# A hybrid decoder trunk on one core: the state space part with one shared phasor table, and each head's gate, norm and output placed among the next head's pieces

## The reference, cut to what matters

```python
def even_mixer(hn, w_in, ...):
    proj = hn @ w_in                       # 2048 -> 512 + 4*1536
    u, q, k, v, g = split(proj)            # 6 retention heads of 256
    y_s5 = s5_mixer(u, ...)                # 32 groups x 64 complex states
    q, k = apply_rope(q), apply_rope(k) * 256 ** -0.5
    o = retention(q, k, v, gamma_log)      # decayed causal scores, 2 chunks of 128
    o = o * rsqrt(mean(o * o, -1) + EPS) * ret_norm
    return concat([y_s5, silu(g) * o]) @ w_out

def s5_mixer(u, ...):
    dt = exp(log_dt); mag = exp(lr * dt)
    ab = mag * (cos(li * dt) + i sin(li * dt))
    bb = f(ab, lr, li) * b
    bu = einsum(u, bb)
    x = associative_scan(x_t = ab * x_{t-1} + bu_t)      # complex
    y = gelu(Re(c x) + d * u)
    return y * sigmoid(y @ glu_w + glu_b)
```

## Time and profile before

| | |
|---|---|
| median of 3 runs | 2261.57 us (2256.18 to 2261.68) |
| the profiled execution | 2257.0 us, span 2255.2 us |
| PE busy | 2162.7 us (96%) |
| DVE busy | 1471.7 us (65%) |
| ACT busy | 1003.2 us (44%) |
| POOL busy | 776.3 us (34%) |
| first matmul of the output projection of layer 0 | 438.62 us |

### The profile page before, as it was taken

How to read it: one execution, slowest core, us unless ns; L and a number is a source line. 1 busy time by engine, 2 the same in 40 slices (tenths; PEclk the granted TensorE clock), 3 DMA queues, 4 the chain that set the end, 5 groups by cost and what they waited for, 6 DMA issues and landing times.

```text
span 2255.2 us, 47390 instructions
## 1 busy us (share of the span) xinstructions
PE 2162.7 (96%) x18426; PEld 2132.9 (95%) x18426; DVE 1471.7 (65%) x1747; ACT 1003.2 (44%) x1244; POOL 776.3 (34%) x880
## 2 busy tenths in 40 slices
PE   8788888999999999999999999999999999999997
PEld 8788777999999999999999989999999999999997
DVE  6378766577666655666666666677666555666666
ACT  4243333444444444444444445545444444444442
POOL 5799995023434300433411000023443101443311
PEclk9899998999999999999999999999999999999999
DMA  6334233454555456555455533455554556554553
GB/s 262 114 135 154 98 135 125 158 201 178 207 200 187 166 193 221 196 194 186 176 187 198 192 125 123 162 192 188 206 187 174 186 193 220 197 187 185 174 197 114
DMA packets 64604, 398.69 MB, mean 177 GB/s; under 512 B 7169, under 2 KB 9729, under 8 KB 29057
## 3 DMA queue, kind: packets, MB, share of 16 engines
q1 hardware_dynamic: 60192, 391.15, 48.2%
q10 hardware_dynamic: 4320, 6.27, 0.8%
HBM read 395.29 MB, written 2.10 MB: 176 GB/s over the span
## 4 chain that ended last, share of the span: by engine, by line
PE 81%; POOLq 9%; POOL 5%; issue 2%; DVE 2%; ACT 1%; DVEq 0%; DMA 0%; ACTq 0%
PE PS L1401 25%; PE PS L1402 25%; PE PS L1405 25%; POOLq L1288 2%; POOLq L1292 2%; POOL g L1290 2%; POOL E L1293 2%; POOLq L1159 2%; POOLq L1166 1%; PE PS L1396 1%; PE PS L1397 1%; PE PS L1398 1%; POOLq L1306 1%; POOL S L1305 1%; PE PS L1751 0%
## 5 line engine op out<-in xcount | busy, mean ns | idle before, releaser
L705 DVE TENSOR_TENSOR lo<-raw,hi 128x1024 fp32r<-128x1024 f32 (+2 forms) x826 | 950.4, 1170 | 527.0 <-ACT hi L356 521.8
L356 ACT ACTIVATE hi<-raw 128x1024 fp32r<-128x1024 f32 (+2 forms) x826 | 785.8, 969 | 722.2 <-PE PS L1405 676.1
L1401 PE MATMUL PS<-XS,hi 128*128 128x256 f32 x3584 | 851.6, 280 | 8.2 <-ACT hi L356 8.2
L1402 PE MATMUL PS<-XS,hi 128*128 128x256 f32 x3584 | 845.4, 278 | 0.0
L1401 PEld LDWEIGHTS PS<-XS,hi 128*128 128x128 f32 x3584 | 680.2, 190 | 15.8 <-issue 15.4
L1402 PEld LDWEIGHTS PS<-XS,hi 128*128 128x128 f32 x3584 | 680.4, 190 | 0.4
L1405 PE MATMUL PS<-XS,lo 128*128 128x256 f32 x3584 | 480.8, 277 | 0.0
L1405 PEld LDWEIGHTS PS<-XS,lo 128*128 128x128 f32 x3584 | 441.5, 188 | 0.0
L1401 PE MATMUL PS<-YF,hi 128*128 128x256 f32 x1408 | 331.8, 276 | 0.0
L1402 PE MATMUL PS<-YF,hi 128*128 128x256 f32 x1408 | 331.8, 276 | 0.0
L1358 POOL TENSOR_TENSOR ctmp<-apad,cws 128x512 f32<-128x512 f32 x88 | 131.9, 1519 | 526.0 <-DVE apad L756 526.0
(11 more groups left out here) (238 smaller groups left out, 2487.7 us busy)
## 6 DMA issues: line engine op xcount, KB each, us to landing
raw<-in_ffn_up SPq DMA_DIRECT2D x176, 1024.0 KB, 4.8
raw<-in_ffn_dn SPq DMA_DIRECT2D x128, 704.0 KB, 4.1
raw<-in_w_in SPq DMA_DIRECT2D x51, 1024.0 KB, 4.9
raw<-in_w_oe SPq DMA_DIRECT2D x16, 1024.0 KB, 4.8
raw<-in_w_oo SPq DMA_DIRECT2D x16, 1024.0 KB, 4.8
raw<-in_mla_dn SPq DMA_DIRECT2D x9, 1024.0 KB, 4.8
raw<-in_w_ukv SPq DMA_DIRECT2D x8, 1024.0 KB, 4.8
raw<-in_w_uq SPq DMA_DIRECT2D x8, 768.0 KB, 4.3
```

The lines of the kernel that those rows point to most:

```text
L356: act.activation(hi[:, p % SLOTS, 0:n], raw[:, u % SLOTS, off:off + n], ACT.Copy).then_inc(hi_ready, 1)
L705: V.tensor_tensor(lo[:, p % SLOTS, 0:n], raw[:, u % SLOTS, off:off + n], f(hi[:, p % SLOTS, 0:n]), ALU.subtract).then_inc(lo_ready, 1)
L1401: mm(PS[:, bank, 0:T], wh, x[:, 0:T], start=first, stop=False)
L1402: mm(PS[:, bank, 0:T], wh, x[:, T:2 * T], start=False, stop=False)
```

## The change

1. The S5 setup is divided: POOL keeps the two exponentials (`s5_magnitude`) and the seven squarings (`s5_powers`); DVE gets the angles, the first phasor, the factor and the scaled B, one part after each of head 0's first four splits. The semaphore `den_ready` goes; `th_ready` and `ph_ready` come.
2. The first 32 steps of all 16 columns' phasors are built once (`first_phasors`, in tiles that share their memory with `acc` and `lot`). `phasors` copies its part and makes levels 5 to 7 only.
3. B's transposes move from G's piece 2 to V's piece 3 of head 0, and ACT's copies of them to behind V's copy.
4. In the S5 heads: b_u(0) and b_u(1) after K's pieces 1 and 2, c_x(0) and b_u(2) after V's piece 1, b_u(3) after V's piece 2, and c_x(1) after K's piece 2 of the next head. DVE makes scan(1) after the second of the next head's K splits. POOL makes rotate_in(0) ahead of the change of sign of C, and C is loaded after bu_copy(1).
5. A head's root, SiLU, norm, output and rounding are taken out of its end and stand in the next head's K stage (`root_and_gate`, `round_y`, `gate_and_variance`, `norm_head`, `head_output`, `y_low`), among the splits of its Q pieces. ACT squares the output after the second K split instead of ahead of all four.
6. The prologue's third and fourth sums of squares stand after piece 4, and the first banks of U are scaled ahead of two splits. `sum_squares` gets one drain.

The diff, cut to its core:

```diff
+        acc, lot = sums[:, 0:2, :], sums[:, 2:4, :]
+        E32 = sums[:, :, :].rearrange("p a t -> p (a t)").rearrange("p (a m n) -> p a m n", a=2, m=KD)
...
# scalar, in even_head
                 for i in range(4):
-                    if h0 == 0 or i:
-                        split(p0 + 4 + i, 16, r)
-                    if s5 and i == 1:
-                        bu_copy(0)
+                    split(p0 + 4 + i, 16, r)
+                    if h0 and i == 0:
+                        root_and_gate(r, h0 - 1)
+                    if s5 and i in (1, 2):
+                        bu_copy(i - 1)
+                    if s5 and i == 2:
+                        load_c()
+                    if glu and i == 2:
+                        act.wait_ge(c_done, 8)
+                        act.dma_start(gluw, A["gluw"]).then_inc(gluw_in, 16)
+                if h0:
+                    round_y(r, h0 - 1)
...
-                act.wait_ge(o_done, H_(1, 1))
-                act.activation(sq[:, :, :], PS[:, 5, :].rearrange("p (a t) -> p a t", a=2), ACT.Square).then_inc(osq_ready, 1)
-
                 for i in range(4):
                     split(p0 + 16 + i, 16, r)
+                    if i == 1:
+                        act.wait_ge(o_done, H_(1, 1))
+                        act.activation(sq[:, :, :], PS[:, 5, :].rearrange("p (a t) -> p a t", a=2),
+                                       ACT.Square).then_inc(osq_ready, 1)
...
# vector
+            root(0)
+            scale_banks(U[:, 0:2, :], 7, 0)
             splits(8, kinds=("std",) * 2)
-            scale_banks(U[:, 0:2, :], 7, 0)
...
                 for i in range(4):
-                    if h0 == 0 or i:
-                        split(p0 + 4 + i, 16, r)
+                    if h0 and i == 0:
+                        gate_and_variance(r, h0 - 1)
+                    split(p0 + 4 + i, 16, r)
+                    if h0 == 0:
+                        (s5_angles, s5_phasor, s5_factor, s5_b)[i]()
+                    if h0 and i == 0:
+                        norm_head(r, h0 - 1)
+                    if h0 and i == 1:
+                        head_output(r, h0 - 1)
+                if h0 > 1:
+                    y5()
+                if h0:
+                    y_low(r, h0 - 1)
                 rotate(KRo, p0 + 4, e0)
...
-                if s5:
-                    scan(1)
...
                 for i in range(4):
                     split(p0 + 16 + i, 16, r)
+                    if s5 and i == 1:
+                        scan(1)
...
# gpsimd
+            def double(e, n, lo_, cos_, sin_):
+                pool.drain()
+                c_, s_ = lo_
+                G.tensor_tensor(c_, e[:, :, :, 0:n], cos_, ALU.mult)
+                G.tensor_tensor(s_, e[:, :, :, 0:n], sin_, ALU.mult)
+                pool.drain()
+                G.tensor_tensor(e[:, 0, :, n:2 * n], c_[:, 0], s_[:, 1], ALU.subtract)
+                G.tensor_tensor(e[:, 1, :, n:2 * n], c_[:, 1], s_[:, 0], ALU.add)
+
+            def first_phasors():
+                G.memset(E32[:, 0, :, 0:1], 1.0)
+                G.memset(E32[:, 1, :, 0:1], 0.0)
+                for l in range(5):
+                    n = 1 << l
+                    c, s_ = (ph[:, l, ri, :].unsqueeze(1).unsqueeze(3).broadcast_to([P, 2, KD, n]) for ri in range(2))
+                    double(E32, n, (g1m[:, :, :, 0:n], g2m[:, :, :, 0:n]), c, s_)
+                pool.drain()
...
             def s5_chunk(h0, r):
+                if h0:
+                    stage(h0, r)
                 phasors(0, h0, r)
-                pool.drain()
+                rotate_in(0, h0, r)
                 pool.wait_ge(cst_in, at(16 * h0 + 16, 16, r))
...
-                rotate_in(0, h0, r)
                 phasors(1, h0, r)
                 rotate_in(1, h0, r)
...
-            pool.wait_ge(den_ready, 1)
-            s5_setup()
+            s5_magnitude()
+            s5_powers()
             pool.wait_ge(bank_free, 2)
             pool.wait_ge(bt_ready, 2)
+            stage(0, None)
+            first_phasors()
             s5_chunk(0, None)
...
# tensor
                 def after_k(i):
-                    if s5 and i == 1:
-                        b_u(0)
+                    if h0 > 1 and i == 2:
+                        c_x(1)
+                    if s5 and i in (1, 2):
+                        b_u(i - 1)
...
-                    if s5:
-                        if i == 1:
-                            c_x(0)
-                            b_u(3)
+                    if s5 and i == 1:
+                        c_x(0)
+                        b_u(2)
+                    if s5 and i == 2:
+                        b_u(3)
+                    if i < 2:
+                        after_q(i + 4)
+                    if i == 3 and h0 == 0:
+                        b_transposed()
...
-                        if s5:
-                            c_x(1)
-                    if i == 2 and h0 == 0:
-                        b_transposed()
```

More of the change, by code:

```diff
@@ L290, in build @@
         cneg_ready = sem("cneg_ready")
-        den_ready = sem("den_ready")
         bu_done = sem("bu_done")
@@ L445, in even_head @@
                     act.activation(U[:, :, :], U[:, :, :], ACT.Gelu_apprx_tanh).then_inc(ge_ready, 1)
-                for i in range(4):
-                    split(p0 + 8 + i, 16, r)
-                    if s5 and i == 0:
-                        bu_copy(1)
+                splits(p0 + 8, 16, r)
                 for i in range(4):
                     split(p0 + 12 + i, 16, r)
-                    if s5 and i < 2:
-                        bu_copy(i + 2)
+                    if s5 and i in (1, 2):
+                        bu_copy(i + 1)
                 act.wait_ge(piece_done, at(p0 + 12, 16, r))
@@ L458, in even_head @@
                 act.activation(Vr[:, 0, :], PS[:, pair(e0 + 2), 0:T], ACT.Copy, scale=rtok[:, 0:1]).then_inc(v_ready, 1)
+                if h0 == 0:
+                    act.wait_ge(bt_psum, 8)
+                    for b in range(2):
+                        act.activation(BT[:, 2 * b:2 * b + 2, :, :].rearrange("p a b c -> p (a b c)"),
+                                       PS[:, 6 + b, :], ACT.Copy).then_inc(bt_ready, 1)
                 if glu:
@@ L495, in _ @@
             even_head(None, 5, False, True)
+            root_and_gate(None, 5)
+            round_y(None, 5)
             def out_projection(n, p0):
@@ L787, in lambda_squared, with tt, ts @@
                 dve.drain()
-                V.reciprocal(pt[:, 12, :], pt[:, 13, :]).then_inc(den_ready, 1)
+                V.reciprocal(pt[:, 12, :], pt[:, 13, :])
+            def tt(o, a, b, op):
+                V.tensor_tensor(o, a, b, op)
+                dve.drain()
+            def ts(o, a, s1, s2, o1, o2=None):
+                if o2 is None:
+                    V.tensor_scalar(o, a, s1, None, o1)
+                else:
+                    V.tensor_scalar(o, a, s1, s2, o1, o2)
+                dve.drain()
@@ new lines, in stt, with s5_angles @@
+            def stt(o, a, s, b, o1, o2):
+                V.scalar_tensor_tensor(out=o, in0=a, scalar=s, in1=b, op0=o1, op1=o2)
+                dve.drain()
+            def s5_angles():
+                th, cs, sn, a, b, c = (col(i) for i in (2, 3, 4, 5, 6, 7))
+                dve.wait_ge(th_ready, 1)
+                ts(a, th, 2.0 / math.pi, MAGIC, ALU.mult, ALU.add)
+                ts(a, a, -MAGIC, None, ALU.add)
+                parts, rest = [], math.pi / 2
+                for bits in (8, 9, 10):
+                    scale = 2.0 ** (bits - 1 - math.floor(math.log2(rest)))
+                    v = math.floor(rest * scale) / scale
+                    parts.append(v)
+                    rest -= v
+                parts.append(rest)
+                stt(b, a, -parts[0], th, ALU.mult, ALU.add)
+                for v in parts[1:]:
+                    stt(b, a, -v, b, ALU.mult, ALU.add)
+                tt(c, b, b, ALU.mult)
+                ts(sn, c, 1.0 / 362880, None, ALU.mult)
+                for k in (-5040, 120, -6):
+                    stt(sn, sn, 1.0 / k, c, ALU.add, ALU.mult)
+                stt(sn, sn, 1.0, b, ALU.add, ALU.mult)
+                ts(cs, c, -1.0 / 3628800, None, ALU.mult)
+                for k in (40320, -720, 24, -2):
+                    stt(cs, cs, 1.0 / k, c, ALU.add, ALU.mult)
+                ts(cs, cs, 1.0, None, ALU.add)
@@ new lines, in s5_b @@
+            def s5_b():
+                B, o, w = (x.rearrange("p a b t -> p (a b t)").rearrange("p (a m c) -> p a m c", a=2, m=KD)
+                           for x in (sB, sT1, sT2))
+                fr, fi = (col(i).unsqueeze(2).broadcast_to([P, KD, 32]) for i in (10, 11))
+                tt(o[:, 0], B[:, 0], fr, ALU.mult)
+                tt(w[:, 0], B[:, 1], fi, ALU.mult)
+                tt(o[:, 0], o[:, 0], w[:, 0], ALU.subtract)
+                tt(o[:, 1], B[:, 1], fr, ALU.mult)
+                tt(w[:, 0], B[:, 0], fi, ALU.mult)
```

(6 more changed lines are left out.)

252 lines of the change are left out of this document (110 added, 142 removed).

## The result

The changed kernel takes **2229.05 us** (median of 4 runs, 2228.34 to 2229.64), against 2260.24 for the kernel before on the same chip: a ratio of 0.9865, with a 95% interval of 0.9848 to 0.9882. It is faster by 31 us; 2205 was forecast, with a range up to 2226. The direction was right, the gain was a little over half of what the sum said, and the time lies 3 us outside the range. The profiled execution has a span of 2226.9 us.

A forecast was written before the change was run, and what follows sets the result against it. POOL's chain was taken to bound the S5 heads, with DVE and POOL blocking each other second. Gains of 14 + 28 + 12 = 54 us bring the profiled 2257.0 to 2203, forecast as 2205 us, range 2182 to 2226.

The forecast's parts named there:

- The setup, step by step: Divided S5 setup: B ready at 64 us, PE waits 6 at V0, POOL starts chunk 0 at about 82.
- the table in front of chunk 0: Shared first phasors on POOL, built once before chunk 0's rotation: about 10 us.
- The mutual blocking: DVE instructions with two SBUF inputs and POOL instructions reading SBUF exclude each other for a whole instruction.
- (d): Steady S5 heads: period falls from 68.4 to 59 us (56 to 62), three periods 28 us less.
- (e): Interleaved heads: c_x(0) held about 3 us, G ends 32.7 after rotate_in(0), 6 us of PE waits per head stay.
- (f): Last head: 53.9 us, so 86.6 from the last rotate_in(0) to the output projection, against 98.4.
- rival 2: S5 heads: new chain longer, POOL waits 5 us more per chunk, period 64 to 65; 2225 us, chance 0.22.
- Rival 1: S5 heads: PE becomes the bound as blocking vanishes with the small POOL operations; 2180 us, chance 0.23.
- 14 + 28 + 12 us: Gains before the output projection: first rotate_in(0) earlier, three shorter periods, shorter stretch after the last rotate_in(0).

The follow-up runs named there:

- e6: Changed kernel with 36 useless matmuls put in front of c_x(0), in the place of PE's wait, in heads 1 to 4; 2217.00 us.
- e3: Changed kernel with levels 5 to 7 of every phasor table left out, so the output is not the reference's; 2192.36 us.
- e14: Changed kernel with the shared table before POOL's wait for B, the second half's last level held until scan(0) ended, and scan(0), c_x(0) one piece later; 2207.64 us.
- e10: Changed kernel with POOL's levels for a chunk's second half held back until scan(0) of the same head has ended; 2218.94 us.
- e12: Changed kernel with the shared table before POOL's wait for B and only the second half's largest level held until scan(0) ended; 2218.18 us.
- e4: Changed kernel with one 1.75 us reciprocal added on DVE in the K stage of heads 1 to 4; 2232.27 us.
- e13: Changed kernel with the reciprocal and Newton step of the heads' norm replaced by one product, so the output is not the reference's; 2211.28 us.
- e7: Changed kernel with scan(0) one V split later on DVE, and c_x(0), b_u(2) and b_u(3) one V piece later on PE; 2224.76 us.

## Why the prediction was right and wrong

**What was right.** That nothing changes from the output projection on. The setup, step by step: PE's wait at head 0's first V piece was put at 6 us and is 5.62; the first rotate_in(0) was forecast to end at 121 and ends at 122.2; the table in front of chunk 0 was called a price. The 121 is partly luck: POOL starts chunk 0 at 86.29 in place of 82 and needs 35.9 us from there in place of 39, so two errors of 3 to 4 us cancel. PE's 15.3 us wait is gone. The mutual blocking was seen and named as what decides.

**What failed is step (d), the period of 59, which measured 64.7, and (e), the layout behind rotate_in(0).** The sum in (d) takes DVE's and POOL's exclusive operations, 64 us less 5 (for the 5 there is no row), as if each would always find the other one's work to run against and never an idle engine. That is the period of a well-packed order, and this order isn't one. POOL idles 14.5 us per head, because rotate_in needs b_u copied, b_u stands behind c_x(0) in PE's queue, and c_x(0) waits for scan(0). DVE idles 6.7 us in V and G. Both are then busy together in the K stage and in scan(0), where blocking is paid on the path. The layout by hand had scan(0) end 7.2 us behind rotate_in(0); it ends 15.2 behind it (246.84 to 262.08): 5.9 because DVE, with the norm and two splits of 2.8 us ahead of it, arrives late, and the rest because scan(0) takes 9.4 beside the levels. In place of (e)'s 3 us wait PE waits 5. In head 4 the four G pieces end at 353.20, 41.6 us behind rotate_in(0) in place of 32.7, and head 5 takes 56.3 us in place of the 53.9 of (f).

**What was missing: the clock.** I allowed 1.5 us for it once, in the setup. It costs 3.3 us in each of the heads with c_x(0) (e6), 12 us in all, half of the miss; without it (e6) the period is 61.5, inside the 56 to 62 of (d). The rows to see it from were in the trace of before: the granted clock of 0.93 in an S5 head, where a share of PE's waits was to remain by my own layout.

**The balance of the miss** in the forecast's own terms, 410.19 less 384.6 = 25.6 us: the first rotate_in(0) +1.2; from it to the last one 189.4 in place of 177, +12.4 (the first of the three steps is 60.0, since scan(0) of chunk 0 ends 10.8 us behind its rotate_in(0), the other two 64.7 and 64.8); from the last one to the output projection 98.6 in place of 86.6, +12.0, of which 8.0 lie before the end of scan(0).

**The rivals.** It is rival 2 that came: POOL waiting for b_u(3) behind V's pieces, scan(0) waiting for a DVE that holds the norm, a period of 64 to 65, 2225 us. These orders of waiting are in the trace, its time is 4 us off, and I gave it 0.22 against 0.50. That the number fits so well is luck in part: it had POOL wait 5 us per chunk, POOL waits 14.5 and isn't the bound, and the rival named neither the stretched scan(0) nor the clock, without which the period is 61.5 (e6). Its weight should have come from the order of the queues, which the diff shows: with the norm put in front of scan(0), and bu_copy behind the splits of V, the period can't be that of free packing. Rival 1 (2180) was refuted as argued: PE's rate is only reached when POOL's levels are gone altogether (e3, 2192).

**And the three terms of the gain?** The sum had 14 + 28 + 12 us for start, periods and last stretch. By the places of the table the changed kernel reaches 5.0 (head 1's scores), 12.2 (three heads) and 11.2 (from head 4's scores to head 5's). The 11.2 are no success of (f): from the end of the last rotate_in(0) to head 4's scores 27.9 us pass (311.60 to 339.46), where it took 16.4 before (340.20 to 356.65). e14 reaches 12.5, 27.6 and 11.1. So a gain of the size forecast was within reach of this kernel, with three more edits; that the terms agree doesn't show that each price was right, since e14 gets there with a wait and a clock loss that the forecast didn't have.

The Trainium skill, "SBUF — State Buffer", section "Who interferes with whom", was used for the exclusion. The runs agree, and add that it isn't a loss to be counted once: e10 has the same instructions on both engines, and DVE's busy time differs by 5.5 us per head according to when POOL works.

## What to carry to other kernels

Work taken from one of two engines that block each other can come back in part as stretched instructions on the other one (here 14.1 us off POOL, 4.8 us onto DVE), unless the order keeps them apart: read both engines' timelines around the operation that the path waits for (here scan(0)), and hold the other engine's early work back until it is past, if that engine idles later anyway. Then look at what comes late by it: in e10 the held levels delayed scan(1), and through the variance, the root and a copy even PE. Price PE's wait together with the pieces behind it, since these may run at the lower clock; where a wait can't be removed, moving it behind another piece of work may take both. And a sum of busy times gives the period of the best order, not of the order written down: before taking it, follow each queue once round the loop.

## What the runs showed of the hardware

Useless matmuls in the place of a 5 us wait of PE made the kernel 12 us faster (e6), with the granted clock of an S5 head at 1.00 in place of 0.92. In head 3 (head 4 for the 1.02) c_x took 1.86 to 1.93 us behind waits of 2.72 (e12), 2.85 (e4) and 5.03 us, and 1.06 behind 0.76 (e6), 1.02 (e14) and 2.06 us (e13); in e7, behind two waits of 3.52 us each, it took 1.73 in one head and 1.06 in another, where the clock fell one step later, in b_u. In e13 it took 1.93 behind a wait of 3.09 us (head 1) and 1.06 behind one of 3.10 us (head 2), and in e14 a wait of 1.67 us before b_u was followed by pieces at the lower level. Which it will be can't be read off the wait alone. A scan of DVE (four of 128x256) took 2.43 us with POOL waiting and 4.09 beside POOL's products of 128x256 and 128x512, so scans are stretched as the two-input additions of the earlier trace rows are. A DVE operation with two SBUF inputs that starts behind a POOL product ends about its own time after that product: in the changed kernel a split that takes 1.16 us alone took 2.96 us (275.95 to 278.91) beside a product that ended at 277.82.
